# Attention masks in rounded f32 instead of bf16, in a two-block transformer on one Trainium2 core

## The chip, the cores and the metric

The kernel is one program on one core of a Trainium2 chip. The metric is the device time of one execution in microseconds (us). The engines are named as in the profile: PE is TensorE (matmuls), PEld its weight loads, DVE VectorE, ACT ScalarE, POOL GpSimd, SP SyncE (here the main issuer of DMAs).

## What is computed

The input is 512 tokens of 1024 features. A first block mixes a stick-breaking attention and a gated linear attention and is followed by an MLP; a second block has a differential attention, an MLP, a short convolution and a last MLP. The change touches the masks of two of these.

```python
def stick_breaking_attention(q, k, v):      # 8 heads of 64
    ...
        z = jnp.einsum('bhtd,bhsd->bhts', q[:, :, start:end], kb) * scale
        past = s_idx < t_idx
        log_beta = jax.nn.log_sigmoid(z)
        log_fail = jnp.where(past, log_beta - z, 0.0)
        later = lax.cumsum(log_fail, axis=3, reverse=True) - log_fail
        w = jnp.where(past, jnp.exp(log_beta + later), 0.0)
        outs.append(jnp.einsum('bhts,bhsd->bhtd', w, vb))

def diff_attention(x, ...):                 # 8 heads, 2 components of 64 each
    ...
        s = jnp.einsum('bqhcd,bkhcd->bhcqk', q_i, k32)
        mask = key_pos[None, :] <= q_pos[:, None]
        s = jnp.where(mask, s, -jnp.inf)
        p = jax.nn.softmax(s, axis=-1)
        a = p[:, :, 0] - lam * p[:, :, 1]
        return jnp.einsum('bhqk,bkhe->bqhe', a, v)
```

## The kernel before

Every f32 product is made from three matmuls of rounded f32 (float32r, shown as f32 in TensorE's lines): each operand is split into a high part (written by ACT) and a low part (written by DVE), and hi x hi, hi x lo and lo x hi are summed in PSUM. Weights come by DMA into `w_raw` (two slots), ACT writes `w_hi`, DVE `w_lo`; a slot comes free when TensorE has used it. All projections and MLPs run so (L689, L701, L714, L739 are their matmuls and transposes).

The order of the work is written out by hand, one program for each engine, joined by semaphores. In the first attention stage, for each of eight heads t, TensorE runs: 4 pieces of a woven projection (`feed`, L813), `sb_sums(t)` (L850, L853), 2 more pieces, `sb_values(t)` (L868) and `sb_scores(t + 1)`. `sb_scores` makes, for each of 4 tiles of keys, three score matmuls (L841, contraction over the 64 features of the head, so 64 rows of the array) and then one mask matmul (L842): the unit matrix as the weights, 128 rows deep, times a 128x128 matrix with -1e30 where a key isn't in the past. It adds the mask to the diagonal tile. The last mask raises `z_ready`. ACT then makes the exponentials and logarithms (L1379, L1381, L1383), DVE and POOL sum them (L1887, L1891, L1893; L573, L576), ACT rounds them (L1393), DVE makes the low part (L1897, `sp_lo`), for which `sb_sums` waits; ACT's L1387 and L1388 and DVE's L1901 lead to `sb_values`. Around head 0 the low-rank gate is made too (L892, L878, L888, gains from DVE L1874), and DVE does the gate's work (L1931 to L1943) in head 2.

In the second attention stage `diff_scores(t)` makes the scores in two halves: in each half 12 score matmuls (L1087, the two components on rows 0 to 63 and 64 to 127) and then four mask matmuls one after the other (L1092). Each half raises `s_mm`; TensorE waits for the first before it begins the second half. DVE's `diff_max` (L2185) and ACT's exponentials (L1533) follow, DVE mixes the two components (L2198), and TensorE turns the result (`diff_turn`, L1103) and multiplies by the values (L1117). Between these it transposes back the output of the head before (`diff_back`, L1125, after ACT's L1547) and runs pieces of the next projections (L1031, L1037, later L1056). In odd heads DVE also makes the rotary embedding of the next pair (L2164 to L2171).

The tiles `ident_b`, `causal_b` and `strict_b` are written once by DVE near the start (L1855 to L1857), from constants loaded by DMA; TensorE waits for them once (`consts_r`, L828).

Of the kernel before, what the change touches and what calls it, by code (L numbers as in the profile page):

```python
# [22 lines left out]
F32R = mybir.dt.float32r  # L23
BF16 = mybir.dt.bfloat16
U8 = mybir.dt.uint8
ALU = mybir.AluOpType
# [3 lines left out]
P = 128  # L30
# [99 lines left out]
def build(nc, w, out):  # L130
    ph, n_quads, n_blocks = plan()
    ctx = ExitStack()
    with ctx:
        def sb(name, shape, dt=F32):
            return ctx.enter_context(nc.sbuf_tensor(name, shape, dt))
# [7 lines left out]
        def sem(name):  # L143
            sems[name] = ctx.enter_context(nc.semaphore(name))
            return sems[name]
# [21 lines left out]
        masks = sb("masks", [P, LEVELS + 1, P], U8)  # L167
        ntri = sb("ntri", [P, P], F32R)
        nones = sb("nones", [P, P], F32R)
        ident_b = sb("ident_b", [P, P], BF16)  # L170
        causal_b = sb("causal_b", [P, P], BF16)
        strict_b = sb("strict_b", [P, P], BF16)


        gains = sb("gains", [P, N_GAINS + 1])
# [5 lines left out]
        psf = ps[:].rearrange("p b n -> p (b n)")  # L181
# [7 lines left out]
        ident = consts[:, K_ID:K_ID + P]  # L189
        strict = consts[:, K_STRICT:K_STRICT + P]  # L190
        b_cum = yf[:, 0:2048]
        tmp = arena[:, 4096:6144]
# [73 lines left out]
        consts_r = sem("consts_r")  # L266
# [148 lines left out]
        def stat_count(name, n, i):  # L415


            _, _, add, _, turn_, _ = junctions[name]
            if add is None:
                return 4 * n + i + 1  # L420
            first = 4 * add
            if turn_ is None:
                return first + i + 1
            if n == add:
                return first + (1 if i == 0 else 2 * i)
            return first + (2 * i + 3 if i < TT - 1 else 2 * TT)
# [96 lines left out]
        def _(pool):  # L523
# [18 lines left out]
            def refine_tiles(name):  # L542
                _, _, add, _, turn_, _ = junctions[name]
                for s_ in range(TT + 1):
                    if add is not None and s_ < TT:
                        refine(name, add, s_)
                    if turn_ is not None and s_ > 0:
                        refine(name, turn_, s_ - 1)
# [95 lines left out]
        def _(pe):  # L644
            mm = nc.tensor.matmul
# [185 lines left out]
            def sb_scores(t):  # L831
                rows = slice(SB_DIM * (t % 2), SB_DIM * (t % 2) + SB_DIM)
                qh, kh, ql, kl = (qk_r[rows, 4 * (t // 2) + n] for n in range(4))
                if t:
                    pe.wait_ge(w_exp, t)

                for j in (0, 1, 3, 2):
                    out_ = z[:, COL[j]:COL[j] + SEQ - P * j]
                    js = slice(P * j, P * (j + 1))
                    for x, (k_, q_) in enumerate(((kh, qh), (kh, ql), (kl, qh))):  # L840
                        mm(out_, k_[:, js], q_[:, P * j:], start=(x == 0 and j != 3), stop=True, skip_group_check=True)  # L841
                    last = mm(out_[:, 0:P], ident_b[:], strict_b[:], start=False, stop=True, skip_group_check=True)  # L842
                last.then_inc(z_ready, 1)

            def sb_sums(t):
# [35 lines left out]
            def gate_up(h):  # L881
# [6 lines left out]
                mm(ps[:, SIDE], w_up16[:, GLA_DK * h:GLA_DK * (h + 1)], low_t, start=True, stop=True).then_inc(up_mm, 1)  # L888

            sb_scores(0)  # L890
            pe.wait_ge(gains_in, GAIN_LOADS * 16)
            nc.tensor.transpose(ps[:, SIDE, 0:N_GAINS], gain_rows[0:N_GAINS], ident[0:N_GAINS, 0:N_GAINS]).then_inc(gains_turned, 1)  # L892
# [5 lines left out]
            for t in range(SB_HEADS):  # L898
                if t:
                    feed(4)  # L900
                sb_sums(t)
                feed(2)
                sb_values(t)
                if t < SB_HEADS - 1:
                    sb_scores(t + 1)
# [52 lines left out]
            for m in range(12):  # L958
                col = SEQ * (m // 3) + P * (m % 3)
                last = nc.tensor.transpose(psf[:, 2048 + P * m:2048 + P * (m + 1)], g_k[:, col:col + P], ident)  # L960
# [46 lines left out]
            for f in range(2):  # L1007
                fs, ts_ = slice(P * f, P * (f + 1)), slice(SEQ // 2, SEQ)
                for k in range(KT):
                    for x, (left, right) in enumerate(((wh, a_hi), (wh, a_lo), (wl, a_hi))):  # L1010
                        last = mm(ps[:, f, ts_], left[:, k, fs], right[:, k, ts_], start=False, stop=True, skip_group_check=True)
# [59 lines left out]
            def diff_scores(t):  # L1071
                u, f = (t // 2) % 2, t % 2
                pe.wait_ge(qk_lo, 2 * (t // 2) + 2)
                if t:
                    pe.wait_ge(pt_lo, t)
                else:
                    pe.wait_ge(turned_lo, turn_base["h_mix1"] + 8)
                if t >= 5:
                    pe.wait_ge(ot_low, 2 * t - 8)
                for steps in (((3, 3), (2, 1)), ((1, 2), (0, 0))):  # L1080
                    for i0, i1 in steps:
                        for x, (zq, zk) in enumerate(((pair_hi, pair_hi), (pair_hi, pair_lo), (pair_lo, pair_hi))):
                            for c, i in enumerate((i0, i1)):
                                rows = slice(DIFF_DIM * c, DIFF_DIM * (c + 1))
                                n = P * (i + 1)
                                starts = x == 0 and (i in (2, 3) or (i, c) == (1, 1))
                                mm(psf[:, DIFF_S[c][i]:DIFF_S[c][i] + n], zq[u][rows, f, P * i:P * (i + 1)], zk[u][rows, 2 + f, 0:n],  # L1087
                                   start=starts, stop=True, skip_group_check=True)
                    for both in steps:
                        for c, i in enumerate(both):  # L1090
                            col = DIFF_S[c][i] + P * i
                            last = mm(psf[:, col:col + P], ident_b[:], causal_b[:], start=False, stop=True, skip_group_check=True)  # L1092
                    last.then_inc(s_mm, 1)
                    if steps[0][0] == 3:
                        pe.wait_ge(s_mm, 2 * t + 1)
# [41 lines left out]
            for t in range(DIFF_HEADS - 2):  # L1137
                diff_scores(t)
                if t:
                    diff_back(t - 1)  # L1140
                project(3)
                diff_turn(t)
                if t == 4:
                    o_turn(0, 5)
                    o_turn(1, 6)
                project(3)
                if t == 5:
                    o_turn(2, 5)
                    o_turn(3, 6)
                diff_values(t)  # L1150
# [3 lines left out]
            for j in range(2):  # L1154
                part(0, j, range(0, 2))
            diff_scores(6)
            diff_back(5)
            for j in range(2):
# [6 lines left out]
            o_turn(5, 6)  # L1165
            diff_values(6)
            diff_scores(7)
            diff_back(6)
            part_piece(1, 1)
# [6 lines left out]
            def rest(blk, j, ks):  # L1176
                s = slot_of(p, blk, 0)
                js = slice(P * j, P * (j + 1))
                for k in ks:
                    for x, (left, right) in enumerate(((ot_hi[k], w_hi), (ot_hi[k], w_lo), (ot_lo[k], w_hi))):  # L1180
                        last = mm(ps[:, 4 * blk + j], left[:, js], right[:, s, k - QUAD], start=(k == QUAD and x == 0),  # L1181
                                  stop=(k == KT - 1 and x == 2))
                return last
# [20 lines left out]
            for j in range(TT):  # L1204
                last = rest(0, j, (7,))
            last.then_inc(quad_done, 1)
            for j in range(TT):
                last = rest(1, j, (6, 7) if j < TT - 1 else (4, 5, 6, 7))
# [454 lines left out]
        def _(dve):  # L1663
            step = Steps(dve, dve_step)
            tt, ts, stt = nc.vector.tensor_tensor, nc.vector.tensor_scalar, nc.vector.scalar_tensor_tensor
# [186 lines left out]
            dve.wait_ge(ident_in, 16)  # L1852
            nc.vector.tensor_copy(ntri[:], consts[:, K_NTRI:K_NTRI + P]).then_inc(consts_r, 1)
            nc.vector.tensor_copy(nones[:], consts[:, K_NONE:K_NONE + P]).then_inc(consts_r, 1)
            nc.vector.tensor_copy(ident_b[:], ident).then_inc(consts_r, 1)  # L1855
            nc.vector.tensor_copy(causal_b[:], tmp[:, 0:P]).then_inc(consts_r, 1)
            ts(strict_b[:], strict, 1.0, 1e30, ALU.subtract, ALU.mult).then_inc(consts_r, 1)  # L1857
            step(nc.vector.tensor_copy(masks[:].rearrange("p a b -> p (a b)"), masks_f))

            def sbq_lo_part(blk, bank0):  # L1860
# [217 lines left out]
            for c in range(1, 3):  # L2078
                dve.wait_ge(st_ready, c)
                dve.wait_ge(st_mm, c)  # L2080
                for h in range(GLA_HEADS):
                    hs = slice(GLA_DV * h, GLA_DV * (h + 1))
                    col = (3072 if c == 1 else 2048) + GLA_DV * h
                    last = stt(g_state[c][:, hs], g_state[c - 1][:, hs], elast[:, 4 * h + c:4 * h + c + 1],
                               psf[:, col:col + GLA_DV], ALU.mult, ALU.add)
# [32 lines left out]
            for i in range(TT):  # L2118
                for half in range(2):
                    dve.wait_ge(turned_hi, turn_base["o_gla"] + 2 * i + half + 1)  # L2120
                    src = ps[:, 6 - 2 * (i % 2) + half].rearrange("p (a b) -> p a b", a=4)
                    for n in range(2):
                        cs = (slice(None), slice(4 * half + n, 4 * half + 4, 2), slice(P * i, P * (i + 1)))
                        last = stt(a_lo[cs], src[:, n:4:2], gains[:, G_GLA + n:G_GLA + n + 1], a_hi[cs].bitcast(F32),
                                   ALU.mult, ALU.subtract)
# [222 lines left out]
```

## Time and profile before

| | us |
|---|---|
| three runs | 2169.66, 2171.01, 2172.4 (median 2171.01) |
| profiled execution, its own time | 2170.88 |
| its span in the trace | 2169.1 |
| PE busy / PEld busy | 2033.6 / 1704.0 |
| DVE / ACT / POOL busy | 1044.3 / 749.1 / 161.8 |
| mean granted TensorE clock | 0.97 of 2.4 GHz |

A busy PE is not PE at its peak: matmuls are pipelined and their ends are modelled. The share of an engine is a mean over stages; whether an added operation costs time is read from the waits and from the chain in the stage in which it runs. A line gives start, duration, engine, source line, operation, tiles and form; `x3` means that three like instructions are merged, and what stands in brackets is idle time of the engine just before, with what ended it ("issue": nothing that the profile shows).

### The profile page before, as it was taken

To read this page: it belongs to the slowest core of one execution; us is meant where nothing else is said; L and a number is where in the kernel's file an instruction comes from. 1 tells how busy PE (TensorE), PEld (TensorE's weight loads), DVE (VectorE), ACT (ScalarE), POOL (GpSimd) and SP (SyncE) were. 2 spreads that over 40 slices of the span, in tenths; PEclk is the share of its full clock that TensorE was granted. 3 is DMA by queue.
4 is the path that set the end of the run, shared out by engine and by line. 5 is a ranking of instruction groups with operands and counts; after the bars stand their busy time and mean duration, and the time that the engine had idled before them with its cause. 6 is when DMAs were issued, how large, how long until landed. Compare 5 with 4: busy or idle time off the path is not lost.

```text
span 2169.1 us, 23378 instructions
## 1 busy us (share of the span) xinstructions
PE 2033.6 (94%) x9821; PEld 1704.0 (79%) x9821; DVE 1044.3 (48%) x957; ACT 749.1 (35%) x866; POOL 161.8 (7%) x327
## 2 busy tenths in 40 slices
PE   6998989999999999989998699999979987999997
PEld 5777768878788888878887588888868766888886
DVE  3346467764542433356775643333452555333434
ACT  3353462424331322345454432232241224231322
POOL 1000033000100000031000300000030012000001
PEclk9999999999999999989999799999989988999999
DMA  4311212222323223222222222322212232222221
GB/s 172 97 57 41 78 39 78 78 78 78 106 99 97 97 97 97 97 73 86 83 64 78 64 96 96 97 96 95 97 60 97 82 111 68 97 97 97 97 97 58
DMA packets 97997, 188.28 MB, mean 87 GB/s; under 512 B 3982, under 2 KB 16288, under 8 KB 97920
## 3 DMA queue, kind: packets, MB, share of 16 engines
q1 hardware_dynamic: 93888, 176.17, 24.7%
q0 software_dynamic: 3744, 10.21, 1.6%
q8 instruction: 58, 0.95, 0.2%
q10 hardware_dynamic: 288, 0.79, 0.1%
q14 instruction: 19, 0.16, 0.0%
HBM read 184.01 MB, written 2.10 MB: 86 GB/s over the span
## 4 chain that ended last, share of the span: by engine, by line
PE 81%; DVE 8%; ACT 4%; POOL 3%; issue 3%; DMA 1%; SPq 0%; POOLq 0%; ACTq 0%; DVEq 0%
PE ps L689 51%; PE ps L813 8%; PE ps L701 5%; PE ps L714 3%; PE ps L1031 2%; PE ps L1037 2%; PE ps L917 1%; POOL small L535 1%; PE ps L739 1%; PE ps L1056 1%; ACT arena L1533 1%; PE ps L1181 1%; ACT w_hi L1230 1%; ACT qk L1295 1%; POOL small L537 1%
## 5 line engine op out<-in xcount | busy, mean ns | idle before, releaser
L1673 DVE TENSOR_TENSOR w_lo<-w_raw,w_hi 128x2048 fp32r<-128x2048 f32 x126 | 288.7, 2292 | 764.6 <-ACT w_hi L1230 764.6
L1230 ACT ACTIVATE w_hi<-w_raw 128x2048 fp32r<-128x2048 f32 x126 | 241.3, 1916 | 874.4 <-PE ps L689 758.4
L689 PE MATMUL ps<-a_hi,w_hi 128*128 128x512 f32 x992 | 386.0, 389 | 0.0
L689 PE MATMUL ps<-a_lo,w_hi 128*128 128x512 f32 x992 | 386.0, 389 | 0.0
L689 PE MATMUL ps<-a_hi,w_lo 128*128 128x512 f32 x992 | 385.9, 389 | 0.0
L689 PE MATMUL ps<-w_hi,h_hi 128*128 128x512 f32 x672 | 263.6, 392 | 11.2 <-DVE h_lo L1717 7.7
L689 PE MATMUL ps<-w_lo,h_hi 128*128 128x512 f32 x672 | 263.1, 391 | 0.0
L689 PE MATMUL ps<-w_hi,h_lo 128*128 128x512 f32 x672 | 262.9, 391 | 0.0
L689 PEld LDWEIGHTS ps<-a_hi,w_hi 128*128 128x128 f32 x992 | 186.3, 188 | 38.6
L689 PEld LDWEIGHTS ps<-a_hi,w_lo 128*128 128x128 f32 x992 | 186.2, 188 | 38.5
L689 PEld LDWEIGHTS ps<-a_lo,w_hi 128*128 128x128 f32 x992 | 186.3, 188 | 38.4
L689 PEld LDWEIGHTS ps<-w_hi,h_hi 128*128 128x128 f32 x672 | 127.1, 189 | 39.0 <-issue 12.4
L689 PEld LDWEIGHTS ps<-w_hi,h_lo 128*128 128x128 f32 x672 | 127.2, 189 | 26.6
L689 PEld LDWEIGHTS ps<-w_lo,h_hi 128*128 128x128 f32 x672 | 127.3, 189 | 26.4
L535 POOL TENSOR_SCALAR small<-small 128x1 f32<-128x1 f32 x44 | 33.3, 756 | 1123.9 <-ACT qk L1295 1121.6
L739 PE MATMUL ps<-consts,y_tm 128*128 128x128 f32 x192 | 39.5, 374 | 77.4 <-DVE y_tm L1803 77.4
L1883 DVE TENSOR_TENSOR w_lo<-w_raw,w_hi 128x2048 fp32r<-128x2048 f32 x36 | 84.0, 2334 | 51.2 <-ACT w_hi L1373 51.0
L1373 ACT ACTIVATE w_hi<-w_raw 128x2048 fp32r<-128x2048 f32 x36 | 68.8, 1911 | 92.4 <-PE ps L813 92.4
L739 PEld LDWEIGHTS ps<-consts,y_tm 128*128 128x128 f32 x192 | 32.1, 195 | 83.6 <-DVE y_tm L1803 42.0
L701 PE MATMUL ps<-w_hi,h_hi 128*128 128x512 f32 x224 | 87.1, 389 | 0.0
L701 PE MATMUL ps<-w_lo,h_hi 128*128 128x512 f32 x224 | 87.1, 389 | 0.0
L701 PE MATMUL ps<-w_hi,h_lo 128*128 128x512 f32 x224 | 87.1, 389 | 0.0
(342 smaller groups left out, 3290.4 us busy)
## 6 DMA issues: line engine op xcount, KB each, us to landing
w_raw<-in_w_ff SPq DMA_DIRECT2D x32, 1024.0 KB, 5.3
w_raw<-in_mlp_w_up SPq DMA_DIRECT2D x32, 1024.0 KB, 5.6
w_raw<-in_mlp_w_down SPq DMA_DIRECT2D x32, 1024.0 KB, 5.1
w_raw<-in_w_in SPq DMA_DIRECT2D x26, 1024.0 KB, 5.0
w_raw<-in_attn_w_qkv SPq DMA_DIRECT2D x12, 1024.0 KB, 5.1
w_raw<-in_conv_w_in SPq DMA_DIRECT2D x12, 1024.0 KB, 5.2
w_raw<-in_w_proj_gla SPq DMA_DIRECT2D x4, 1024.0 KB, 5.1
w_raw<-in_w_out SPq DMA_DIRECT2D x4, 1024.0 KB, 5.0
```

The lines of the kernel that those rows point to most:

```text
L535: pstep(nc.gpsimd.tensor_scalar(v, ss, 1.0 / D, EPS, ALU.mult, ALU.add))
L689: last = mm(ps[:, bank0 + j], left, right, start=(k == 0 and x == 0), stop=(k == QUAD * quads - 1 and x == 2), skip_group_check=halves)
L701: last = mm(ps[:, bank0 + j], left, right, start=False, stop=(a == QUAD - 1 and x == 2))
L714: last = mm(ps[:, bank0 + j, ts_], left[:, s, k, js], right[:, k, ts_], start=(half == 0 and k == 0 and x == 0), stop=False, skip_group_ch ...
L739: last = nc.tensor.transpose(ps[:, tile_bank(name, i, half), P * a:P * (a + 1)], y_tm[:, i, P * k:P * (k + 1)], ident)
L813: last = mm(ps[:, j], left, right, start=(k == 0 and x == 0), stop=(k == QUAD * quads - 1 and x == 2))
L1031: last = mm(ps[:, bank], left[:, k, fs], right[:, k], start=(k == 0 and x == 0), stop=(k == KT - 1 and x == 2))
L1037: last = mm(out_, left[:, k, js], right[:, k], start=(c % 2 == 0 and k == 0 and x == 0), stop=True, skip_group_check=True)
L1230: nc.scalar.activation(w_hi[:, s], w_raw[:, s], ACT.Copy).then_inc(hi_ready, 1)
L1373: nc.scalar.activation(w_hi[:, s], w_raw[:, s], ACT.Copy).then_inc(hi_ready, 1)
L1673: tt(w_lo[:, s], w_raw[:, s], w_hi[:, s].bitcast(F32), ALU.subtract).then_inc(lo_ready, 1)
L1883: tt(w_lo[:, s], w_raw[:, s], w_hi[:, s].bitcast(F32), ALU.subtract).then_inc(lo_ready, 1)
```

## The change

The three tiles are held as rounded f32 (F32R), like the operands of the scores, and carry new names. The mask matmuls read them in place of the bf16 ones. Three DVE operations write f32r instead of bf16. The number of instructions and their order stay as they are.

```diff
-        ident_b = sb("ident_b", [P, P], BF16)
-        causal_b = sb("causal_b", [P, P], BF16)
-        strict_b = sb("strict_b", [P, P], BF16)
+        ident_r = sb("ident_r", [P, P], F32R)
+        causal_r = sb("causal_r", [P, P], F32R)
+        strict_r = sb("strict_r", [P, P], F32R)
...
-                    last = mm(out_[:, 0:P], ident_b[:], strict_b[:], start=False, stop=True, skip_group_check=True)
+                    last = mm(out_[:, 0:P], ident_r[:], strict_r[:], start=False, stop=True, skip_group_check=True)
...
-                            last = mm(psf[:, col:col + P], ident_b[:], causal_b[:], start=False, stop=True, skip_group_check=True)
+                            last = mm(psf[:, col:col + P], ident_r[:], causal_r[:], start=False, stop=True, skip_group_check=True)
...
-            nc.vector.tensor_copy(ident_b[:], ident).then_inc(consts_r, 1)
-            nc.vector.tensor_copy(causal_b[:], tmp[:, 0:P]).then_inc(consts_r, 1)
-            ts(strict_b[:], strict, 1.0, 1e30, ALU.subtract, ALU.mult).then_inc(consts_r, 1)
+            nc.vector.tensor_copy(ident_r[:], ident).then_inc(consts_r, 1)
+            nc.vector.tensor_copy(causal_r[:], tmp[:, 0:P]).then_inc(consts_r, 1)
+            ts(strict_r[:], strict, 1.0, 1e30, ALU.subtract, ALU.mult).then_inc(consts_r, 1)
```

## Rows read from the trace of the kernel before

**Rows 1.** The page: busy time and share of an engine; chain by engine.
```profile
PE 2033.6 (94%) x9821; PEld 1704.0 (79%) x9821; DVE 1044.3 (48%) x957; ACT 749.1 (35%) x866; POOL 161.8 (7%) x327
...
PE 81%; DVE 8%; ACT 4%; POOL 3%; issue 3%; DMA 1%; SPq 0%; POOLq 0%; ACTq 0%; DVEq 0%
```

**Rows 2.** Timeline of TensorE in scores of head 1: start us, us, engine, line.
```profile
133.85 0.41 PEld L841 LDWEIGHTS ps<-qk_r 64*128 64x128 f32 x3
133.86 0.55 PE L841 MATMUL ps<-qk_r 64*128 64x128 f32 x3
134.33 0.10 PEld L842 LDWEIGHTS ps<-strict_b,ident_b 128*128 128x128 bf16 x1
134.34 0.23 PE L842 MATMUL ps<-strict_b,ident_b 128*128 128x128 bf16 x1
134.49 0.41 PEld L841 LDWEIGHTS ps<-qk_r 64*128 64x128 f32 x3
...
135.04 0.20 PEld L813 LDWEIGHTS ps<-a_hi,w_hi 128*128 128x128 f32 x1
135.08 0.48 PE L813 MATMUL ps<-a_hi,w_hi 128*128 128x512 f32 x1
```

**Rows 3.** Timeline of TensorE where the first scores follow a projection, 92.6 us.
```profile
92.61 0.39 PE L689 MATMUL ps<-w_hi,a_lo 128*128 128x512 f32 x1
92.92 0.29 PEld L841 LDWEIGHTS ps<-qk_r 64*128 64x128 f32 x2 [0.35 <-issue]
```

**Rows 4.** Timeline in narrow windows: a mask, and single matmuls after a drain.
```profile
133.70 0.23 PE L842 MATMUL ps<-strict_b,ident_b 128*128 128x128 bf16 x1
133.86 0.32 PE L841 MATMUL ps<-qk_r 64*128 64x128 f32 x1
92.92 0.49 PE L841 MATMUL ps<-qk_r 64*128 64x512 f32 x1
118.44 0.50 PE L813 MATMUL ps<-a_hi,w_hi 128*128 128x512 f32 x1
```

**Rows 5.** Waits of TensorE, 90 to 300 us: us in total, times, longest.
```profile
PE ps L850 <- DVE h_hi L1897: 6.5, 5, 4.0
PE ps L878 <- DVE gains L1874: 3.2, 1, 3.2
```

**Rows 6.** Chain that ended last, in order of time, 90 to 300 us.
```profile
135.11 0.18 PE ps L842
...
146.49 0.85 PE ps L850 x3
...
158.45 1.23 DVE y_tm L1931
```

**Rows 7.** Timeline of a differential head: one group of masks.
```profile
1016.92 0.40 PE L1092 MATMUL ps<-causal_b,ident_b 128*128 128x128 bf16 x4
```

**Rows 8.** Differential heads: loads of L1125 behind a group, and TensorE's waits.
```profile
1018.38 0.23 PEld L1092 LDWEIGHTS ps<-causal_b,ident_b 128*128 128x128 bf16 x4
1018.72 0.66 PE L1125 MATMUL ps<-consts,qk 128*128 128x128 f32 x4
1027.81 0.75 PEld L1103 LDWEIGHTS ps<-consts,arena 128*128 128x128 f32 x7 [0.31 <-DVE arena L2198]
1066.77 0.42 PEld L1125 LDWEIGHTS ps<-consts,qk 128*128 128x128 f32 x4 [1.14 <-ACT qk L1547]
1164.56 0.23 PEld L1092 LDWEIGHTS ps<-causal_b,ident_b 128*128 128x128 bf16 x4
1164.74 0.42 PEld L1125 LDWEIGHTS ps<-consts,qk 128*128 128x128 f32 x4
```

**Rows 9.** Durations of DVE's copies at the start, rounded f32 and bf16.
```profile
L1854 DVE CAST nones<-consts x1: 219/219/219, 34.8 to 34.8; 128x128 fp32r<-128x128 f32 x1
L1855 DVE CAST ident_b<-consts x1: 217/217/217, 34.9 to 34.9; 128x128 bf16<-128x128 f32 x1
```

**Rows 10.** Busy time, granted clock (PEclk), DMA share of one stretch.
```profile
90.00:300.00 210.00, 197.95 (x884) 155.60 (x883) 104.42 (x88) 99.26 (x69) 14.36 (x34) 0.97 0.18 57
```

## The prediction

> **What bounds the kernel now.** I read the page first: the matmul side of TensorE is busy 94% of the span, and the chain that ended last lies on it for 81%, with VectorE at 8% and ScalarE at 4% [rows 1]. So a nanosecond added to TensorE's stream counts unless TensorE then stands in front of a wait that ends at its old time. The changed matmuls run in two stages only: 32 masks of stick-breaking attention (L842) between 93 and 290 us, and 64 masks of the differential attention (L1092) between 994 and 1165 us. In the order of reading: the timeline of one head around each mask, the waits of TensorE in both stages, and the chain in order of time, which tells for each head whether the masks lie on it. The reader should look at starts of loads (PEld), not at matmul durations, since a matmul's time includes its passage through the array.
>
> **What a mask costs now.** The bf16 load takes 0.10 us where three rounded-f32 loads beside it take 0.41 together, each begun 0.11 after the one before, so about 0.19 each (as one of the projection does, 0.20) [rows 2]. In a head of L842 three things are to be seen. First, the mask's load at 134.33 starts only 0.07 us before the last score matmul (ending at 134.41) has left the array: it doesn't slip under it. Second, the next score load, at 134.49, again starts 0.07 us before the mask ends at 134.57. Third, where the mask is followed by a projection (L813, 128 rows deep like the mask), its load at 135.04 starts at once, beside the mask's own [rows 2]. Is this drain a matter of format or of depth? The scores use 64 rows, the masks 128. The first score load after a projection, f32 after f32 with depths 128 and 64, starts at 92.92, 0.08 us before the matmul in front (92.61 + 0.39) ends [rows 3]; and bf16 to f32 at equal depth doesn't drain (third point above). So depth decides, format doesn't, and the change keeps every drain.
>
> **Part 1, the isolated masks (L842).** After a drain the bf16 mask takes 0.23 us from load to end [rows 2]. The nearest row for what it becomes is a score matmul of 128 columns in rounded f32, also after a drain: 0.32 us (133.86) [rows 4]. That is 0.09 more. Two 512-column ones after a drain, 64 and 128 rows deep, take 0.49 and 0.50 [rows 4], so depth adds up to 0.01: I take 0.095 each, with 0.09 to 0.10 as bounds. Four masks: z_ready, for which ScalarE's L1379 waits, comes 0.38 us later. TensorE itself loses 0.36: three masks at 0.095, and behind the fourth the projection's first matmul, which now ends 0.52 after the mask's load starts (135.04 to 135.56), ends 0.59 after it (0.11 for each of the two loads, then its own 0.37), 0.07 more.
> Which heads pay? The waits say that TensorE stood before sb_sums (L850) for sp_lo in five heads, 6.5 us in all, 4.0 of it once [rows 5]. In heads 1, 4, 5 and 6 the chain runs through the last mask (135.11) and ScalarE, VectorE and GpSimd to L850 at 146.49 [rows 6]: they pay 0.38 each. In heads 3 and 7 there is no wait and TensorE's own stream is the chain: 0.36 each. Head 2 has the wait of 4.0 us: VectorE's gate work from 158.45 holds the chain there, begun before its masks end [rows 6], so it pays nothing, as long as those 4.0 us stand. Head 0 pays nothing either: TensorE waits 3.2 us for the gains (L1874) right behind it [rows 5]. Sum: 4 x 0.38 + 2 x 0.36 = 2.2 us, bounds 1.9 (0.09 a mask, half of one head absorbed) and 3.0 (all eight heads).
>
> **Part 2, the masks in groups of four (L1092).** The first follows a drain: +0.095. The other three follow each other at equal depth: four bf16 matmuls take 0.40 us, so 0.06 apart [rows 7]. In rounded f32 the load of 128 columns sets the step: 0.11, as the score loads show (three in 0.41) [rows 2]. So +0.05 each, +0.15 for three, and 0.25 a group; the bounds for the three are 0 (if repeated loads of the same unit matrix cost nothing) and 0.17. A head has two groups: 0.50 us. Behind the first TensorE waits for its own s_mm before the second set of scores; that wait only moves. Queued behind it are all of TensorE's later matmuls, and VectorE's diff_max waits for s_mm too.
> Which heads pay? In even heads and in heads 6 and 7 the chain goes from the masks straight on: 5 x 0.50 = 2.5 us. In the odd heads 1, 3, 5 the rotary work of VectorE sets the time, up to the wait that ends at 1027.81 [rows 8]. Their masks sit inside, and TensorE has slack twice: before diff_back (L1125), where the load follows the group's start by 0.34 us against 0.18 in an unhindered head, so 0.16 of slack, and in one head a wait of 1.14; then before diff_turn (L1103), idle 0.31 [rows 8]. Of 0.50, 0.43 to 0.50 vanish: 0.1 us is left for all three together. Sum 2.6 us, bounds 2.0 and 4.0 (nothing absorbed).
>
> **Part 3, edits with one answer.** The DVE copies into the new tiles at the start: rounded f32 217 to 219 ns like bf16 [rows 9], so nothing. The tiles grow by 3 x 256 bytes a partition; no transfer or order changes, no DMA is touched, and the number of instructions stays. PSUM addresses and the accumulation stay.
>
> **A rule weighed against the rows.** The load rows show 0.10 us for bf16 and about 0.19 for rounded f32 [rows 2]. The Trainium skill ("TensorE: Matmul & The Clock Gate", section "Weight-path perf modes") says that a fast load of 128 weights is used when the type isn't FP32, with 32 cycles for it in theory; its section on LDWEIGHTS gives columns / 1.2, 107 ns for an ordinary one. The trace agrees in kind, and its 0.11 spacing agrees in size. By that page the difference would be 80 ns for an isolated mask (an estimate from it), and the whole would be some 4.3 us in place of 4.8.
>
> **The sum.** 2.2 + 2.6 = 4.8 us. The profiled execution took 2170.88 us (span 2169.1), 0.13 below the median 2171.01, so the two are alike: 2171.0 + 4.8 = 2175.8 us.
>
> **Rivals.**
> - A, nothing is absorbed: heads 0 and 2 and the odd heads pay too, 3.0 + 4.0 = 7.0 us, 2178.0. For it: TensorE is busy 94%. Against: the waits of 4.0, 3.2, 1.14 and 0.31 us [rows 5, 8], which end by other work. 14%.
> - B, the drain hangs on format when the depth grows (64 to 128): then a rounded-f32 mask would slip under the scores at the 0.11 step and not after 0.16; L842 would gain 0.05 a mask, 0.2 a head, 1.3 us in six heads; the groups would gain 0.05 and lose 0.15, +0.5 in five heads. 2170.2. The rows have the drain for equal format only in the direction 128 to 64 [rows 3]. 9%.
> - C, faster, the same mechanism both ways: equal format lets loads pass in both directions. The 0.25 us from a mask's end (133.93) to the end of the next, narrowest score (134.18) [rows 4] would fall to 0.11 as well: with 0.05 from each mask some 0.7 us gained a head, 4.2 in six heads, less 0.5 for the groups, so 2167.3. It decides as soon as the two loads at 134.33 and 134.49 come earlier. Against it stands the load at 92.92 [rows 3]. 6%.
> - D, each mask in a group drains the one before it. The Trainium skill, same page, section "Part 3: Packing small matmuls", says that loads overlap with running matmuls only if their row groups differ. The rows don't bear it out for equal depth (bf16 masks 0.06 apart, the projection's load beside the mask) [rows 2, 7]. Priced by rows: a step of 0.25 (0.16 + 0.09) in place of 0.11, 0.14 x 6 = 0.8 more a head, paid in eight heads less the slack, so some 6 us on top: 2182. 3%.
> - E, the masks hide wholly, or the shift is won back where the clock differs: the granted clock is 0.97 over 90 to 300 us [rows 10], so some 12 us there run at 1.2 GHz and not 2.4, and where such stretches fall may move by what is added. The three runs of before spread by 2.7 us. 2172 to 2173. 13%.
>
> **How the numbers follow.** The forecast of my sum has 55%, around 2175.8; its own range, by the bounds 1.9 + 2.0 and 3.0 + 4.0 and the spread of runs, is 2174 to 2178.5. The range given must leave out no more than 2 in 10: low 2172.3 takes in E, high 2179.5 takes in A with a run 1.5 us up; B, C and D stay outside. About 0.2% (4.3 us, the least that can be told from no change here) puts the line at 2175.3 on one side and 2166.7 on the other: slower by more has 0.55 (0.38 of the forecast's 0.55, with A and D), within it 0.40 (the forecast's other 0.17, E, B, and 0.01 of C), faster 0.05 (C, which lies at that line).
>
> **What would show it.** In the changed profile L842's load should take about 185 ns and its matmul about 0.32 us; the loads before and after it should still start 0.07 us before the end of what is in front. A group of L1092 should take about 0.66 us against 0.40. The wait of 4.0 us at head 2 should shrink by about 0.4, and the waits of L1103 and L1125 in odd heads should go. If a mask's load starts beside running score matmuls, B or C holds. If z_ready is 0.38 later in every head and the stages still end at their old times, absorption was underrated. The forecast is wrong if a rounded-f32 matmul of 128 columns and 128 rows costs more than its 64-row neighbour suggests.

## The result, and the profile after

The change makes the kernel slower: a median of 2179.9 us over 12 executions (2175.2 to 2188.4) against 2170.5 us over 12 of the kernel before (2168.3 to 2172.9), a ratio of 1.0046 with an interval of 1.0032 to 1.0060. That is 9.4 us where 4.8 were forecast, and just outside the range (2179.5). The profiled execution of the changed kernel took 2175.22 us with a span of 2173.4, 0.6 below the forecast. So one execution shows the forecast nearly to the point, and the median shows twice the size: the study is about that gap.

The page of the kernel after, as [rows 1] (busy time; chain by engine):

```profile
PE 2039.1 (94%) x9821; PEld 1709.2 (79%) x9821; DVE 1044.6 (48%) x957; ACT 749.8 (34%) x866; POOL 162.3 (7%) x327
...
PE 82%; DVE 7%; ACT 4%; POOL 3%; issue 3%; DMA 1%; SPq 0%; POOLq 0%; ACTq 0%; DVEq 0%
```

The masks themselves, durations in ns (min/median/max):

```profile
L842 PEld LDWEIGHTS ps<-strict_r,ident_r x32: 186/186/186, 92.6 to 291.9; 128*128 128x128 f32 x32
L842 PE MATMUL ps<-strict_r,ident_r x32: 326/326/329, 92.6 to 291.9; 128*128 128x128 f32 x32
L1092 PE MATMUL ps<-causal_r,ident_r x64: 273/276/328, 995.0 to 1169.3; 128*128 128x128 f32 x64
```

The timeline of the kernel after in the scores of head 1, the same place as [rows 2] (matmuls, then loads), and one group of four masks, as [rows 7]:

```profile
134.28 0.33 PE L842 MATMUL ps<-strict_r,ident_r 128*128 128x128 f32 x1
134.53 0.62 PE L841 MATMUL ps<-qk_r 64*128 64x256 f32 x3
135.08 0.33 PE L842 MATMUL ps<-strict_r,ident_r 128*128 128x128 f32 x1
135.25 0.44 PE L813 MATMUL ps<-a_hi,w_hi 128*128 128x512 f32 x1
...
134.28 0.19 PEld L842 LDWEIGHTS ps<-strict_r,ident_r 128*128 128x128 f32 x1
134.53 0.41 PEld L841 LDWEIGHTS ps<-qk_r 64*128 64x128 f32 x3
135.08 0.19 PEld L842 LDWEIGHTS ps<-strict_r,ident_r 128*128 128x128 f32 x1
135.19 0.19 PEld L813 LDWEIGHTS ps<-a_hi,w_hi 128*128 128x128 f32 x1
...
1018.09 0.66 PE L1092 MATMUL ps<-causal_r,ident_r 128*128 128x128 f32 x4
```

An isolated mask now ends 0.33 us after its load starts, against 0.23. The score load behind it (134.53) still comes 0.08 before the mask's end (134.28 + 0.33): the drain is there although all formats are now equal. The projection's load follows the last mask's by 0.11, and its first matmul ends at 135.69, 0.61 after the mask's load starts (0.52 before, 0.59 forecast). A group of four takes 0.66 us against 0.40. All of this is as forecast.

The waits of TensorE in the kernel after, 90 to 300 us, beside [rows 5]:

```profile
PE ps L850 <- DVE h_hi L1897: 6.3, 5, 3.7
PE ps L878 <- DVE gains L1874: 2.9, 1, 2.9
```

The long wait at head 2 shrank from 4.0 to 3.7, that at head 0 from 3.2 to 2.9: there the added time is absorbed. Where the time went in this execution, and in a longer one of the same kernel (run `again`, below), is seen from the starts of the first score matmul of some heads (us, from the timelines; the last line is the span):

| | before | after | again |
|---|---|---|---|
| stick-breaking scores of head 1 | 131.9 | 131.7 | 132.5 |
| scores of head 2 | 156.0 | 156.2 | 159.6 |
| scores of head 7 | 286.8 | 288.5 | 295.0 |
| differential scores of head 0 | 992.9 | 993.6 | 1001.4 |
| scores of head 6 | 1139.1 | 1141.1 | 1148.8 |
| scores of head 7 | 1161.7 | 1165.8 | 1173.6 |
| span | 2169.1 | 2173.4 | 2181.3 |

In `after` a head of the first stage grows by 0.4 us. `again` takes 3.0 us more than before between heads 1 and 2 alone (27.0 against 24.1), with the same instructions as `after`. The granted clock tells why. Busy time, then the granted clock (0.93 and the like), DMA share and GB/s, of 131 to 156, 188 to 213, 285 to 311 and 1139 to 1162 us, TensorE only (the number behind `x` counts matmuls); first the kernel before:

```profile
131.00:156.00 25.00, 24.75 (x121) 1.00 0.16 55
188.00:213.00 25.00, 25.00 (x112) 0.93 0.17 56
285.00:311.00 26.00, 26.00 (x118) 0.93 0.13 41
1139.00:1162.00 23.00, 19.17 (x117) 1.00 0.14 46
```

The kernel after, profiled execution:

```profile
131.00:156.00 25.00, 24.73 (x119) 1.00 0.15 50
188.00:213.00 25.00, 25.00 (x109) 0.93 0.17 58
285.00:311.00 26.00, 25.73 (x120) 1.00 0.20 68
1139.00:1162.00 23.00, 20.43 (x108) 0.93 0.14 46
```

The same kernel, execution `again`:

```profile
131.00:156.00 25.00, 25.00 (x104) 0.86 0.16 57
188.00:213.00 25.00, 23.59 (x97) 0.86 0.19 63
285.00:311.00 26.00, 26.00 (x108) 0.87 0.13 41
1139.00:1162.00 23.00, 20.43 (x127) 0.94 0.25 91
```

TensorE's clock has two levels, 1.2 and 2.4 GHz, and a mean of 0.86 over 25 us means that 28% of them ran at the lower. In the kernel before the lower level stands behind the scores of heads 3 and 7 (0.93), not behind those of head 1. In `again` there is more of it in all three windows of the first stage, though not all of it behind scores: one stretch, at 189.9 us, comes before the scores of head 3, which begin there at 192.7. Nor does all of it in the kernel before: its other two stretches in the first stage, at 99.1 and 174.2 us, stand behind TensorE's waits of 3.2 and 4.0 us, and the one behind head 3 also follows a wait of 2.3 us that ended 2.1 us before those scores.

The stretch in the second stage has another place. In `after` it begins at 1151.3 us, 0.7 us behind the end of TensorE's longest wait there, between heads 6 and 7:

```profile
PE ps L1056 <- ACT y_tm L1564: 2.5, 1, 2.5
```

The kernel before has the same wait, word for word, and no half clock behind it. The granted clock recorded in each trace gives the time at the lower level by stage (us of half clock, twice what is lost by it; one execution each):

| | 0 to 312 | 312 to 985 | 985 to 1190 | from 1190 |
|---|---|---|---|---|
| before | 13.7 | 37.5 | 0 | 82.0 |
| plain, pad, grouped_bf16, grouped_again | 13.7 | 34.1 | 0 | 82.1 |
| after, only_stick, dense_add | 13.7 | 34.1 | 3.4 | 82.1 to 82.6 |
| again | 30.7 | 34.1 | 3.4 | 82.0 |
| extra_drain | 23.9 | 34.1 | 3.4 | 82.1 |
| only_diff, grouped_f32r, group_look | 17.1 | 34.1 | 3.4 | 82.1 to 82.6 |
| diff_look | 13.7 | 34.1 | 10.2 | 82.6 |
| diff_drain | 13.7 | 34.1 | 3.4 | 88.7 |

So the profiled executions of before and after have the same half-clock time in all, 133 us, at other places: after has 3.4 us more in the second stage and 3.4 less near 590 us. That is why their spans differ by little more or less than what the masks themselves take.

### The profile page after: what moved, and what is told of

It reads as the page before. It is cut to its first block, busy times and chain, and to the rows that moved or that the text cites. A ratio compares the mean times of both kernels' runs of the same rounds, so it can differ in the third digit from the quotient of the medians.

```text
span 2173.4 us, 23378 instructions
## 1 busy us (share of the span) xinstructions
PE 2039.1 (94%) x9821; PEld 1709.2 (79%) x9821; DVE 1044.6 (48%) x957; ACT 749.8 (34%) x866; POOL 162.3 (7%) x327
## 4 chain that ended last, share of the span: by engine, by line
PE 82%; DVE 7%; ACT 4%; POOL 3%; issue 3%; DMA 1%; SPq 0%; POOLq 0%; ACTq 0%; DVEq 0%
PE ps L689 51%; PE ps L813 8%; PE ps L701 5%; PE ps L714 3%; PE ps L1031 3%; PE ps L1037 2%; PE ps L917 1%; POOL small L535 1%; PE ps L1056 1%; PE ps L1087 1%; PE ps L1181 1%; ACT w_hi L1230 1%; PE ps L739 1%; ACT qk L1295 1%; POOL small L537 1%
```

## The experiments

For each execution the mean granted clock is known. The span times (1 - clock) is the time lost to the lower level, if all of it had been TensorE's to use; the rest is the time at equal clock. One execution is uncertain by 1.1 us, since the clock is given to three digits; means are better. The split has a bias: a matmul that is slower while TensorE would have waited anyway costs nothing, so "lost to clock" is at most what the clock costs, and "rest" at least what the instructions take. The 12 executions of before that were timed with `after` are recorded without their clocks, apart from the profiled one, so `after` is compared with the other groups of before. All values in us:

```
kernel          n   median   mean     lost to clock   rest     mean clock
before         17   2168.2   2169.2   64.1            2105.0   0.9704   (beside again to grouped_bf16)
before         33   2170.0   2170.3   65.0            2105.3   0.9700   (beside grouped_f32r to plain)
before         15   2170.3   2170.8   65.8            2105.0   0.9697   (beside dense_add)
before          9   2170.2   2170.1   64.3            2105.8   0.9703   (beside diff_drain)
after          12   2179.9   2180.6   71.0            2109.6   0.9674
again           6   2179.7   2179.4   69.7            2109.7   0.9680
only_stick      8   2174.6   2175.0   67.6            2107.4   0.9689
only_diff       9   2173.6   2174.5   68.1            2106.4   0.9687
grouped_bf16    5   2161.7   2162.2   63.1            2099.1   0.9708
grouped_again   5   2163.4   2162.8   64.0            2098.8   0.9704
grouped_f32r   11   2171.7   2171.6   69.6            2102.0   0.9679
extra_drain    11   2173.3   2174.6   68.0            2106.6   0.9687
dense_add      11   2173.9   2173.8   65.0            2108.8   0.9701
diff_drain      5   2175.6   2177.0   70.5            2106.5   0.9676
pad            11   2169.8   2169.6   64.0            2105.5   0.9705
plain          11   2169.5   2169.8   65.0            2104.8   0.9700
```

**The changed kernel again** (no edit).

> The changed kernel once more, for the spread of its executions. The theory of the sum: in every execution the masks cost the 4.3 us that the two profiled spans differ by (2173.4 against 2169.1); what goes beyond it, up to 2188, is stretches at 1.2 GHz that only some executions have, so the longer an execution, the lower its mean granted clock: 0.970 at 2175 and 0.964 at 2188. The rival: the format itself costs more in some executions at the same clock; then time and clock don't go together. Expected: times from 2175 to 2188, clock falling by about 0.001 for each 2 us.

Times and clocks go together: 2174.9 at 0.970, 2178.5 at 0.968, 2183.2 at 0.966. At equal clock all six lie between 2108.8 and 2111.1. The split of the change: 4.7 us at equal clock (2109.7 - 2105.0), 5.6 us to the clock (69.7 - 64.1). Here and below, a range given "by the spread" is the difference of two means with two of its standard errors on either side: 2.2 to 9.0 for this 5.6. The rival, a format that costs more in some executions at one clock, falls.

**One stage at a time.**

```diff
# only_stick: L842 alone (only_diff: L1092 alone, likewise with causal_r)
-        strict_b = sb("strict_b", [P, P], BF16)
+        ident_r = sb("ident_r", [P, P], F32R)
+        strict_r = sb("strict_r", [P, P], F32R)
...
-                    last = mm(out_[:, 0:P], ident_b[:], strict_b[:], start=False, stop=True, skip_group_check=True)
+                    last = mm(out_[:, 0:P], ident_r[:], strict_r[:], start=False, stop=True, skip_group_check=True)
```

> Rounded f32 for the masks of the stick-breaking attention alone (L842), bf16 for the others, with one more copy of the unit matrix. The sum gives 2.2 us above the kernel before. If the half-clock stretches of the changed kernel come from this stage, executions up to 10 us longer appear here too (median 5 us or more above before); if they come from the differential stage, the executions stay within 3 us of each other.

> Rounded f32 for the masks of the differential attention alone (L1092), bf16 for the others. The sum gives 2.6 us above the kernel before, with a narrow spread. If the half-clock stretches come from this stage, its executions spread by 10 us and the median lies 6 us or more above before.

Ratios 1.0028 (1.0018 to 1.0039) and 1.0024 (1.0014 to 1.0033). At equal clock +2.4 and +1.4 (forecast 2.2 and 2.6), to the clock +3.5 and +4.0. By the spread both additions to the clock are clear of zero (1.5 to 5.5 and 2.2 to 5.8). So the added half-clock time comes with either stage's masks; the choice between the two stages that I had set up was not one. It doesn't always lie in the stage that was changed: the trace of only_diff has 3.4 us of it more than before in the first stage, where its masks are bf16.

**Side effects of the edit.** Two unused tiles that together have the size that the change adds, and one more copy, with the masks as before; and the kernel before itself.

```diff
+        spare_r = sb("spare_r", [P, P], F32R)
+        pad = sb("pad", [P, 64])
...
+            nc.vector.tensor_copy(spare_r[:], ident).then_inc(consts_r, 1)
```

> The kernel before with nothing of the change but its side effects: 768 bytes a partition more in front of the small tiles, and one more copy of the unit matrix by VectorE at the start. If the addresses or the copy had a part in the result, it shows here; the theory of the sum and of the clock says no difference: ratio 1.000 within 0.1%, clock 0.971.

> The kernel before once more, unchanged, as a null of the comparison and for the spread of its mean clock: 2167.5 to 2172.6, most at 0.971, and another trace of it: where its half-clock stretches lie should be seen behind scores and waits of the first stage, as in the trace before, but not always at the same ones.

Both 0.9999 (0.9990 to 1.0008). Addresses and copies have no part in it. But `plain` also shows executions from 2167.6 at 0.971 to 2172.8 at 0.968: the kernel before has this spread too, only less of it.

**Masks in a group, bf16.** One drain in front of four masks in place of four.

```diff
-                    last = mm(out_[:, 0:P], ident_b[:], strict_b[:], start=False, stop=True, skip_group_check=True)
+                for j in (0, 1, 3, 2):
+                    last = mm(z[:, COL[j]:COL[j] + P], ident_b[:], strict_b[:], start=False, stop=True, skip_group_check=True)
```

> The kernel before with bf16 masks, but in sb_scores all twelve score matmuls first and then the four masks one after the other, so that one drain in front of the masks is left in place of four and three behind them go. By the starts of before a head's scores take 0.85 us less (three masks at 0.16 and three returns that cost 0.14 to 0.20 more than an undrained step, against three steps of 0.06). With six of eight heads paying, as in the forecast, 5 us less: about 2165.5. If the drain hangs on something other than the change of depth, no change. If the saving is given back in clock, less than 2 us.

> grouped_bf16 once more, for its size and its clock: a scores stretch of 2.5 us in place of 3.3. If a shorter thin stretch keeps the clock up, the mean clock is 0.970 or above in all executions and the times stay within 4 us: 2160 to 2164.

The timeline of grouped_bf16 in one head (all twelve scores, then the masks L843):

```profile
211.49 2.19 PE L841 MATMUL ps<-qk_r 64*128 64x512 f32 x12
...
213.61 0.40 PE L843 MATMUL ps<-strict_b,ident_b 128*128 128x128 bf16 x4
```

The scores take 2.5 us (211.49 to 214.01) against 3.3. Ratios 0.9964 (0.9952 to 0.9977) and 0.9962 (0.9949 to 0.9976): 5.9 and 6.2 us at equal clock, 1.0 and 1.8 from the clock, which is at 0.970 or above in all ten executions. This beats both kernels. I had 5 us; the drains cost about what the starts said. Whether their removal also brings clock back isn't settled: the 1.0 is within its spread of 1.9, the 1.8 just outside its 1.7.

**Masks in a group, rounded f32** (the same edit on the changed kernel), and a second trace of it.

> The changed kernel (all masks in rounded f32) with the masks of sb_scores behind the twelve score matmuls. A head's scores then take 2.5 us + 0.25 (0.095 for the first mask, 0.05 for each of the next three), against 3.3 with isolated bf16 masks and 3.7 with isolated rounded-f32 ones. Theory 1, the added half-clock stretches come from the thin stretch of the scores growing longer, whatever the format: the stretch is now shorter than before, so the clock stays at 0.970 to 0.971 in most executions, and the time is that of grouped_bf16 (2161.7) plus 1.3 in the first stage and 2.6 in the second: 2165.5. Theory 2, the format itself lowers the clock: 0.966 to 0.968 in half of the executions and a median of 2169 or more.

> Another trace of grouped_f32r, of which all eleven executions were at 0.967 or 0.969. If the clock falls in the differential stage, its half-clock time between 985 and 1180 us is 3 us or more, against 0 in the trace of before; the rest should lie in the first stage behind sb_scores.

1.0008 (0.9999 to 1.0017). At equal clock 2.9 to 3.2 us above the grouped bf16 kernels, where 3.9 were expected. But the clock is at 0.967 or 0.969 in all eleven executions, which I hadn't expected, and the median is 2171.7 where theory 1 had 2165.5. The first stage alone can't be it. Both traces of this kernel have a half-clock stretch at 1145 us and in the first stage one at 275 us, of which the traces of grouped_bf16 have neither (the one at 275 isn't particular to rounded f32: `plain` has one at 277.5); the second trace took 2169.0 us. By this run alone theory 2, the format, would have stood. Against the kernel before it loses 4.6 us to the clock, not clearly more than only_diff (4.0), which has the same masks in the second stage.

**Length or format, first stage.** A bf16 mask more, at a place where it drains twice; and a like amount of time added by dense work. (The dense matmuls stand at the head of `sb_values`, so twelve others, about 2 us, lie between them and the scores.)

```diff
# extra_drain
                         mm(out_, k_[:, js], q_[:, P * j:], start=(x == 0 and j != 3), stop=True, skip_group_check=True)
+                        if j == 1 and x == 0:
+                            mm(out_[:, 0:P], ident_b[:], strict_b[:], start=False, stop=True, skip_group_check=True)
# dense_add
+                    for _ in range(2 if j == 0 else 0):
+                        mm(ps[:, SIDE, 0:], sbv_hi[:, 0, vs], sb_whi[:, ws], start=True, stop=True, skip_group_check=True)
```

> The kernel before, all bf16, with one mask more in each head of sb_scores, put between the first and the second score matmul of the second key tile, where it drains the array twice (0.16 to its end, some 0.2 for the return): the scores of a head take about 0.35 us more, as the rounded-f32 masks made them (0.38). The mask is added twice there, which leaves the weights at zero. The sum gives 5 to 6 heads x 0.35 = 1.9 us. Theory 1 (a longer thin stretch): the clock falls as in only_stick, some executions at 0.967 to 0.969, median 5 to 6 us above before. Theory 2 (the format): clock 0.971 as before, median 2 us above before.

> The kernel before, bf16, with two more 512-column matmuls of full depth in each head, right in front of sb_scores (the first product of sb_values three times instead of once, each overwriting the one before). They stand back to back with like ones, so the head grows by 2 x 0.23 = 0.45 us, about what the rounded-f32 masks add (0.38), at the same place on the path, but the thin stretch of the scores stays 3.3 us long. Time at the same clock: 5 to 6 heads x 0.45, +2.5 us. Theory 1 (the thin stretch's length makes the half-clock stretches): mean clock as before, median 2172.5. Rival (any change of the spacing between the heads does it): clock 0.967 to 0.969 in half of the executions, as in extra_drain, median 2175 or more.

The extra mask (134.56) in the timeline of extra_drain, first stage:

```profile
134.19 0.44 PE L841 MATMUL ps<-qk_r 64*128 64x384 f32 x1
134.56 0.23 PE L843 MATMUL ps<-strict_b,ident_b 128*128 128x128 bf16 x1
134.72 0.62 PE L841 MATMUL ps<-qk_r 64*128 64x384 f32 x2
```

extra_drain: 1.0018 (1.0008 to 1.0027); +1.3 us at equal clock, +3.0 to the clock, 7 of 11 executions at 0.969 or below. It holds no rounded-f32 mask. Theory 1 had the median 5 to 6 us above before; it is 3.3 above (the mean 4.3). dense_add: 1.0013 (1.0004 to 1.0022); +3.8 us at equal clock (2.5 expected), more than twice as much, and nothing to the clock (65.0 against 65.8): no execution of 11 below 0.970. So in this stage neither a rounded-f32 mask nor the mere shift of the heads is needed: a longer stretch of thin matmuls and drains brings half-clock time, added time in dense matmuls doesn't. By the spread the 3.0 us may be 0.5 to 5.5, and the -0.8 of dense_add -2.2 to 0.6; the two ran on different chips, each beside executions of before. Which of the two does it, the length of the stretch or the number of its drains, isn't separated: extra_drain adds both. The windows of extra_drain in its profiled execution, as above:

```profile
131.00:156.00 25.00, 25.00 (x112) 0.93 0.20 71
285.00:311.00 26.00, 26.00 (x113) 0.91 0.14 44
```

Those of dense_add:

```profile
131.00:156.00 25.00, 24.74 (x117) 1.00 0.21 75
285.00:311.00 26.00, 25.75 (x122) 1.00 0.18 60
```

**Length or format, second stage.** The four bf16 masks of a half in two pairs, no instruction added.

```diff
-                    for both in steps:
-                        for c, i in enumerate(both):
+                        for c, i in enumerate((i0, i1)):
```

> The kernel before, all bf16, with the four masks of each half of diff_scores split in two pairs: two masks behind the first pair of score tiles, two behind the second. No instruction is added; each half has one more drain in front of masks (+0.11) and one behind (+0.14 to 0.20), so a half takes about 0.27 us more, as the rounded-f32 masks made it (0.25). At the same clock +1.4 us, as only_diff (the odd heads absorb theirs). Theory 1 (a longer thin stretch brings half-clock stretches, in this stage as in the first): mean clock 0.9685 to 0.969, median 2173 to 2175. Theory 2 (in this stage it is the format): clock 0.970, median 2171.5.

> Another trace of only_diff, for the places of its half-clock stretches. Theory 1: one at about 1150 us as in its first trace (0.98 mean granted clock over that stage, against 1.00 before). If it has none there and the mean is still below 0.970, they lie elsewhere, and the place is a matter of the execution.

diff_drain: 1.0036 (1.0022 to 1.0049); +0.7 us at equal clock and +6.2 to the clock (4.9 to 7.5), all five executions at 0.967 or 0.968, with bf16 masks. In this stage too the format isn't needed. That it is the thin stretch isn't shown here: no run adds dense work to this stage. In the trace of diff_drain only 3.4 us of the added half clock lie in the stage; 6.8 us more lie behind 1190 us, in code that nobody changed. Its window, and two of diff_look (rounded f32):

```profile
1139.00:1162.00 23.00, 20.20 (x112) 0.93 0.13 46
```

```profile
1139.00:1162.00 23.00, 20.21 (x112) 0.93 0.13 46
1161.00:1180.00 19.00, 17.65 (x91) 0.82 0.18 56
```

The stretch near 1150 us stands in every trace of a kernel with time added to TensorE's stream (nine: after, again, only_stick, only_diff, extra_drain, dense_add, grouped_f32r, its second look, diff_drain; diff_look makes ten) and in none of the five of before, plain, pad and the two grouped bf16 ones. Three of the ten (only_stick, extra_drain, dense_add) have the second stage untouched. In all ten it begins within 1 us of the end of TensorE's wait of 2.5 us for L1564, not behind scores; only the second stretch of diff_look (0.82) stands behind those of head 7. So its place depends also on how the time before it shifted, and dense_add shows that this one alone isn't what makes the loss: it has it and loses nothing in the mean.

## Why the prediction was wrong

- **The drain (depth, not format): right.** With equal formats the loads still start 0.07 to 0.08 us before the end in front. Rivals B and C fall.
- **Part 1: right.** 0.096 us a mask (326 against 230 ns). From the scores of head 1 to those of head 7 the profiled kernel became 1.9 us longer, as the forecast for heads 1 and 3 to 6 (4 x 0.38 + 0.36 = 1.9); head 2 by nothing. At equal clock only_stick gives 2.4 (2.2 forecast).
- **Part 2: right by the traces.** 0.66 against 0.40 us. In the profile heads 0, 2 and 4 became longer by 0.50, 0.54 and 0.55, heads 1 and 5 by 0.10 and 0.13. Head 3 became 0.55 shorter: its chain holds the DMA of the rotary swap, 3.02 us long in the trace before and 2.45 after, with which I hadn't reckoned. only_diff gives 1.4 at equal clock, not 2.6, but the DMA isn't the missing 1.2: in its trace head 3 takes 25.0 us, as before. There the time from the scores of head 0 to those of head 7 is 172.7 us against 168.8; without the 1.7 us that the half-clock stretch between them costs, and with the 0.5 of head 7, that is 2.7 us (2.4 in diff_look). So the forecast holds in the stage, and the 1.4 shows how low the rest at equal clock can come out. The length of head 3 doesn't hang on the masks either: in dense_add, with bf16 masks, it is 24.2. The line of the chain after:

```profile
1059.68 2.45 DMA qk<-y_tm
```

- **Rival A: wrong, though its 2178.0 lies nearest to the median.** The time is absorbed where the sum had it: the waits at heads 2 and 0 shrank by 0.3 us each, head 2 of the first stage became no longer, and of the loads' waits in the second stage that for L1125 (1.1 us) is gone and those for L1103 fell from 0.9 to 0.3.
- **Rival D: wrong, as given.** The masks in a group follow each other at 0.11, not 0.25.
- **The rule weighed: the trace decides.** The Trainium skill ("TensorE: Matmul & The Clock Gate", section "Weight-path perf modes") gave me an estimate of 80 ns for an isolated mask, from the 32 cycles that its row of theory gives for fp8; measured are 96. By the page 4.3 us in all, by the rows 4.8, at equal clock 4.7 was measured (again, against 2105.0) and 4.3 (after, against 2105.3). They can't be told apart in the total.
- **The step that failed: the clock, rival E.** I took it for a disturbance of either sign ("where such stretches fall may move by what is added") and gave it no size in the sum. It is one-sided: every kernel with longer thin stretches lost more to the clock in the mean, 3.0 to 6.2 us against the executions beside it, and none lost less. In the trace of before the windows with 0.93 stand behind scores of heads 3 and 7; that there is something to lose could have been read, its size couldn't. Measured 5.6 to 6 us (lost to clock 69.7 and 71.0 against 64.1 and 65.0), as much as the whole sum or more. The upper end of the range (rival A and 1.5 us) had no such term either. The sum at equal clock was right, and so was the sign; the size was half. That the profiled execution came so near the forecast was luck of the draw: it is the fastest of the twelve.

What stays open: why the clock falls behind a given head and not another; whether in the second stage it is the thin stretch at all, since dense work was added in the first stage only; and why a group of rounded-f32 masks of 0.25 us more in the second stage costs as much clock as 0.38 a head in the first. That the format adds nothing of its own to the clock isn't shown either, only that the loss comes without it. The traces show places in single executions only, and the executions of one kernel differ.

## What to carry to other kernels

Cost an added TensorE operation twice: once by the sum at equal clock, once by what it does to the stretch in which it stands. If that stretch is thin (small matmuls, array drained between depths) and the trace shows half-clock time behind such stretches already, lengthening it can cost clock on top, as each of the added masks and drains did here; added time in dense matmuls cost none in the one place where it was tried. A single profiled execution doesn't show this: compare the mean clock of many. Put matmuls of equal depth together: moving four masks behind twelve scores was worth 0.36 to 0.38%, more than the format of the same masks (0.28%).

## What was not expected of the hardware

- A load of other depth than the matmul in front (64 and 128 rows, both directions) starts only 72 ns before that matmul ends by the profile (ends are modelled), in bf16 and in rounded f32; a load of equal depth starts at once or at a step of 0.11 us (rounded f32) or 0.06 us (bf16).
- Executions of one program differ by up to 13 us (2175.2 to 2188.4), some 10 of them through the granted clock: at equal clock the twelve executions of after lie between 2107.6 and 2110.9.
- Added dense work (dense_add) left the executions more alike: 2171.8 to 2174.5 in eleven, against 2167.7 to 2173.5 in fifteen of before beside them.
